# A mixture-of-experts stage with split weights, a fixed first block for each expert, and GpSimd at work on the output weights

## The reference, cut to what matters

```python
probs = softmax(ht @ w_router); sel = probs + b_router     # 512 x 16
# the best of 4 groups of experts, then the best two experts in it: e_idx, gate_w
def expert_block(args):
    xb, e = args
    return (silu(xb @ w1[e]) * (xb @ w3[e])) @ w2[e]       # w1, w3: 1024 x 512, w2: 512 x 1024
# each token's two results, weighted by gate_w, are added
```

## Time and profile before

| | |
|---|---|
| median of 3 runs | 3185.82 us (3181.49 to 3186.29) |
| the profiled execution: its own time | 3187.43 us |
| its span | 3185.7 us |
| PE busy | 2728.6 us (86%) |
| DVE, ACT, POOL busy | 1517.8, 946.5, 61.4 us |
| mean granted TensorE clock | 0.906 of full |

### The profile page before, as it was taken

The page is one execution under the profiler, slowest core; times in us unless marked ns, Lnnn a source line. Parts: engine busy times, 40 slices in busy tenths (PEclk is TensorE's granted clock), DMA queues, the critical chain, the costliest instruction groups (busy, mean ns, idle before and its releaser), DMA issues. The chain is left out here.

```text
span 3185.7 us, 32864 instructions
## 1 busy us (share of the span) xinstructions
PE 2728.6 (86%) x12575; PEld 1996.8 (63%) x12575; DVE 1517.8 (48%) x2296; ACT 946.5 (30%) x1497; POOL 61.4 (2%) x161
## 2 busy tenths in 40 slices
PE   7999799678887899389999478899999666899998
PEld 6777687556665775344444234578887665778886
DVE  6778435545656574311111444463344885453334
ACT  4333222224434322111111223353232323353233
POOL 0000000000000000100000100000000000000000
PEclk8999699889887999599999788899999887999999
DMA  7667343211210740088888201123232112222330
GB/s 241 212 218 240 130 155 143 86 53 47 53 34 27 272 151 1 31 325 309 324 304 301 83 26 43 57 71 101 93 101 71 16 30 80 80 79 93 93 106 27
DMA packets 304736, 390.75 MB, mean 123 GB/s; under 512 B 23560, under 2 KB 211451, under 8 KB 304348
## 3 DMA queue, kind: packets, MB, share of 16 engines
q1 hardware_dynamic: 295196, 354.33, 33.7%
q0 software_dynamic: 6960, 25.70, 2.1%
q10 hardware_dynamic: 2448, 8.91, 0.7%
HBM read 361.11 MB, written 27.80 MB: 122 GB/s over the span
## 5 line engine op out<-in xcount | busy, mean ns | idle before, releaser
L2887 PE MATMUL banks<-big,tail_w_parts 128*128 128x512 f32 x1920 | 442.9, 393 | 16.9 <-DVE tail_w_parts L3044 16.9
L2887 PEld LDWEIGHTS banks<-big,tail_w_parts 128*128 128x128 f32 x1920 | 363.3, 189 | 95.0 <-DVE tail_w_parts L3044 17.5
L2887 PE MATMUL banks<-h_parts_second,tail_w_parts 128*128 128x512 f32 x1440 | 333.1, 392 | 12.8 <-DVE h_parts_second L3069 12.8
L1264 PE MATMUL banks<-h_parts,ssm_w_parts 128*128 128x512 f32 x984 | 267.1, 433 | 61.6 <-DVE ys_plain L1535 26.6
L2887 PEld LDWEIGHTS banks<-h_parts_second,tail_w_parts 128*128 128x128 f32 x1440 | 272.5, 189 | 71.2 <-issue 14.4
L3044 DVE TENSOR_TENSOR tail_w_parts<-w_second,tail_w_parts 128x2048 fp32r<-128x2048 f32 x70 | 160.3, 2292 | 283.2 <-ACT tail_w_parts L2948 283.2
L1264 PEld LDWEIGHTS banks<-h_parts,ssm_w_parts 128*128 128x128 f32 x984 | 205.2, 212 | 119.8 <-DVE ssm_w_parts L1514 42.5
L2341 PE MATMUL banks<-w,experts_xt 128*128 128x512 f32 x544 | 238.9, 597 | 0.9 <-DVE experts_xt L2388 0.9
L2948 ACT ACTIVATE tail_w_parts<-w_second 128x2048 fp32r<-128x2048 f32 x70 | 133.8, 1914 | 265.4 <-PE banks L2887 265.3
L2341 PEld LDWEIGHTS banks<-w,experts_xt 128*128 128x128 f32 x544 | 104.2, 192 | 132.6 <-issue 132.6
L601 PE MATMUL banks<-h_parts,ssm_parts 128*128 128x512 f32 x576 | 135.8, 398 | 14.8 <-DVE ssm_parts L590 11.6
(11 more groups left out here) (606 smaller groups left out, 3812.7 us busy)
## 6 DMA issues: line engine op xcount, KB each, us to landing
w_second<-in_mlp_w_dram SPq DMA_DIRECT2D x64, 1024.0 KB, 5.1
w<-in_w_exp_gate_dram SPq DMA_DIRECT2D x17, 2048.0 KB, 8.9
w<-in_w_exp_up_dram SPq DMA_DIRECT2D x17, 2048.0 KB, 8.8
w<-in_w_exp_down_dram SPq DMA_DIRECT2D x17, 2048.0 KB, 10.8
w<-in_w_in_dram SPq DMA_DIRECT2D x65, 512.0 KB, 3.9
w<-in_mod_mix_w_dram SPq DMA_DIRECT2D x24, 1024.0 KB, 5.0
w<-in_mod_ffn_w_dram SPq DMA_DIRECT2D x24, 1024.0 KB, 5.0
w<-in_w_in_dram SPq DMA_DIRECT2D x16, 1024.0 KB, 6.9
```

The costliest lines, as they stand in the source:

```text
L1264: mm = pe.matmul(ps[:, t % 2, :], parts[:, t % SPLITS, w, kk, :], k.hp[:, x, kk, :], start=(kk == 0 and j == 0), stop=(kk == KD - 1 and j ...
L2887: mm = pe.matmul(ps[:, bank(n, f), :], w_part(n, w)[:, kk, f * P:(f + 1) * P], x[:, v, kk, :], start=(first_chunk(n) and kk == 0 and j == ...
```

## The change

The routing becomes one stage, and the experts' loop is written out for 16 experts, with all of their weights split.

- The router's weights and the six 1 MB halves of expert 0 are loaded during `norm_mix`. The logits are formed in `norm_ffn_in` behind each tile of `h` (8 products of 512 columns, 16 rows of output). The ranks come from `rank_entries`: five operations for all pairs at once.
- Expert n has row p of its first block at row `p * NBLK + n` of one DRAM tensor, `k.rows`; rows over 128 go to spill blocks behind these (`NBLK` = 24). POOL scatters the rows of `h` themselves (8 indirect transfers of 0.5 MB). x of expert n is then a plain load by SP; y is stored to the place of x.
- Each expert has six halves of weights: 0, 1 gate; 2, 3 up; 4, 5 down. Each half has one raw slot in `k.w` and one split slot (`parts`). ACT makes the high parts; DVE makes the low parts of 0 to 3, and POOL those of 4 and 5. A raw slot is loaded again once its low part is made.
- Spill blocks (one here) are done after the 16 experts by the old loop in plain f32, with plain loads.

The core of it (`wait_low` waits for the low part of half h of expert n; `done` is the order of the high parts):

```diff
+    def load(self, sp, n, h):
+        if n:
+            self.wait_low(sp, n - 1, h)
+        ...
+        sp.dma_start(self.raw(h)..., src...).then_inc(self.raw_loaded[h], 16)
+    def high(self, act, n, h):
+        act.wait_ge(self.raw_loaded[h], 16 * (n + 1))
+        if n and h < 4:
+            act.wait_ge(self.up_used, 4 * (n - 1) + h + 1)
+        elif n:
+            act.wait_ge(self.down_used, 2 * (n - 1) + h - 3)
+        act.activation(self.high_part(h), self.raw(h), ACT.Copy).then_inc(self.high_done, 1)
+    def low(self, eng, n, h):
+        eng.wait_ge(self.high_done, self.done[n, h])
+        eng.tensor_tensor(self.low_part(h), self.raw(h), self.high_part(h).bitcast(F32),
+                          ALU.subtract).then_inc(self.low_done if h < 4 else self.down_low, 1)
+    def products(self, pe, n, h, out, x, first, start, stop):
+        self.wait_low(pe, n, h)
+        for kk in range(KE):
+            for j, (v, w) in enumerate(((0, 0), (0, 1), (1, 0))):
+                mm = pe.matmul(out, x[:, v, first + kk, :], self.tile(h, w, kk), ...)
+        mm.then_inc(self.up_used if h < 4 else self.down_used, 1)

 experts_stage:
 sync:
+            for n in range(NE):
+                if 1 <= n and n + 1 < NE:
+                    for h in range(4):
+                        m.load(sp, n + 1, h)
+                if n + 2 < NE:
+                    sp.wait_ge(s["x_turned"], n + 1)
+                    m.load_x(sp, n + 2)
+                if n + 1 < NE:
+                    for h in (4, 5):
+                        m.load(sp, n + 1, h)
 gpsimd:
-                pool.indirect_dma_start(xg[:], None, m.h_rows, ...)
+            for n in range(NE):
+                for half in range(2):
+                    m.low(pool, n, 4 + half)
 tensor:
+            def down(n):
+                pe.wait_ge(s["hidden_low"], n + 1)
+                if n:
+                    pe.wait_ge(s["y_copied"], 2 * n)
+                for half in range(2):
+                    m.products(pe, n, 4 + half, ps[:, 5 + half, :], ht, 0, True, True)
+            turn(0)
+            for n in range(NE):
+                pe.wait_ge(s["x_low"], n + 1)
+                for slot in range(2):
+                    for h in range(2):
+                        m.products(pe, n, 2 * slot + h, ps[:, 2 + slot, :], xt, h * KE, h == 0, h == 1)
+                if n + 1 < NE:
+                    turn(n + 1)
+                if n:
+                    down(n - 1)
+                pe.wait_ge(s["hidden_done"], n + 1)
+                ...                                 # four transposes of hidden
+            down(NE - 1)
+            pe.wait_ge(s["y_copied"], 2 * NE)
 scalar:
+            high_x(0)
+            for n in range(NE):
+                if n:
+                    high_hidden(n - 1)
+                if n + 1 < NE:
+                    m.high(act, n + 1, 0)
+                    m.high(act, n + 1, 1)
+                act.wait_ge(m.up_used, 4 * n + 2)
+                act.activation(sig[:], ps[:, 2, :], ACT.Sigmoid).then_inc(s["sig_done"], 1)
+                if n + 1 < NE:
+                    m.high(act, n + 1, 2)
+                    m.high(act, n + 1, 3)
+                    high_x(n + 1)
+                for half in range(2):
+                    m.high(act, n, 4 + half)
+                    if n:
+                        copy_y(n - 1, half)
+                if n:
+                    store_y(n - 1)
+            ...                                     # the last expert, then a wait for the stores of y
 vector:
+            low_x(0)
+            for n in range(NE):
+                if n:
+                    low_hidden(n - 1)
+                if n + 1 < NE:
+                    m.low(dve, n + 1, 0)
+                    m.low(dve, n + 1, 1)
+                dve.wait_ge(s["sig_done"], n + 1)
+                dve.tensor_tensor(t[:], ps[:, 2, :], sig[:], ALU.mult).then_inc(s["gated"], 1)
+                if n + 1 < NE:
+                    m.low(dve, n + 1, 2)
+                ...
+                dve.tensor_tensor(hidden[:], t[:], ps[:, 3, :], ALU.mult).then_inc(s["hidden_done"], 1)
+                if n + 1 < NE:
+                    m.low(dve, n + 1, 3)
+                    low_x(n + 1)
+            low_hidden(NE - 1)
```

`high_x`, `low_x`, `high_hidden` and `low_hidden` split the turned x (128x1024, from PSUM) and the turned hidden (128x512, from PSUM) in the same way. The routing stage ends with SP's loads:

```diff
+            sp.wait_ge(m.scattered, 16 * 2 * TB)
+            m.load_x(sp, 0)
+            for h in range(2):
+                m.load(sp, 1, h)
+            m.load_x(sp, 1)
+            for h in range(2, 4):
+                m.load(sp, 1, h)
```

More of the change, by code:

```diff
@@ L495, in _ @@
             k.clear(sp)
+            if experts and not logits:
+                experts.load_router(sp)
+                for h in range(EH):
+                    experts.load(sp, 0, h)
         @block.tensor
@@ L504, in _ @@
                 sum_channels(k, pe, lambda c: pe.wait_ge(s["out_done"], c + 1))
+            if logits:
+                pe.wait_ge(experts.router_loaded, 32)
+                for c in range(KD):
+                    pe.wait_ge(s["out_done"], c + 1)
+                    pe.matmul(ps[0:NE, 2, :], experts.wr[:, c, :], dst[:, c, :], start=(c == 0), stop=(c == KD - 1))
         @block.vector
@@ L2053, in _, with rank_entries @@
                                                   op1=ALU.add))
-def router_stage(k, chosen, share):
+EH = 6
+HALVES = 2 * KE
+def rank_entries(step, dve, rank, above, even, val, later):
+    shape = [P, val.shape[1], EG, EG]
+    mine = val.rearrange("p g (n o) -> p g n o", o=1).to_broadcast(shape)
+    other = val.rearrange("p g (o n) -> p g o n", o=1).to_broadcast(shape)
+    step(dve.tensor_tensor(above, other, mine, ALU.is_gt))
+    step(dve.tensor_tensor(even, other, mine, ALU.is_equal))
+    step(dve.tensor_tensor(even, even, later.rearrange("p (o n) m -> p o n m", o=1).to_broadcast(shape), ALU.mult))
+    step(dve.tensor_tensor(above, above, even, ALU.add))
+    step(dve.tensor_reduce(rank, above, AX.X, ALU.add))
@@ L2071, in _ @@
             k.clear(sp)
[L2072 to L2130, removed]
-            assert step.n == ROUTER_STEPS, step.n
@@ L2192, in _ @@
             for b in range(TB):
[L2193 to L2199 removed]
+                mm = pe.transpose(ps[:, 1, b * NE:(b + 1) * NE], lt[:, b * P:(b + 1) * P], k.ident[0:NE, 0:NE])
@@ L2271, in experts_stage @@
+            step(dve.tensor_reduce(plan_f[:, 0:SPILL], passed[:], AX.X, ALU.add))
+            step(dve.tensor_scalar(plan_f[:, 0:SPILL], plan_f[:, 0:SPILL], float(NE - 1), None, ALU.min))
+            step(dve.tensor_copy(plan_f[:, SPILL:], end[0:1, NE - 1:NE]))
+            step(dve.tensor_copy(m.plan[:], plan_f[:]))
+            for h in range(4):
+                m.low(dve, 0, h)
 def experts_stage(k, m):
```

459 lines of the change are left out of this document (270 added, 189 removed).

## The result

The changed kernel takes 3256.66 us (median of 4 runs, 3253.82 to 3257.05), the kernel before 3186.06 on the same chip (3181.49 to 3188.05). The ratio is 1.022, with an interval of 1.020 to 1.024: slower by 70 us. The forecast was 3235, the range 3165 to 3300.

The account below looks back on a forecast made before the run. PE bounded the old loop at 23.2 us a block; a ring of 29.2 us a period would bound the new one. Expert 0 at 1322.6, rounds to 1744.8 and spill block at 1785.6 put the end 48.5 us later: 3235, range 3165 to 3300.

Parts of the forecast that it names:

- a ring: Experts' loop: SP's loads, ACT's high parts and POOL's low parts follow one another, a period of 29.2 us; forecast's chance 75%.
- Rival (c): Experts' loop: the ring is not closed; transfers or PE set a period of 19 us, total 3102; chance 7%.
- Rival (b): Experts' loop: POOL's low part is cheap; below 2.85 us the kernel is faster, at 2.29 it takes 3170; chance 5%.
- (e): Experts' loop: PE falls to the low clock in its pauses and stays there, 36 us a period, total 3341; chance 5%.
- Rival (d): Experts' loop: POOL and DVE block each other on each low part, 6.7 us each, 68 more, total 3303; chance 8%.
- In front of the loop: From the norm to expert 0's first product: that product starts at 1322.6, 40.7 us earlier than before.
- The logits' products: In the norm: eight products follow the tiles of h, 7.13 us from the second tile on, ending at 1284.4.
- the scatter: In front of the loop: 8 x 0.5 MB through POOL's queue take 15.1 us, with 12 and 25 as ends.
- x of expert 0: In front of the loop: its load takes 2.6 us, by the fastest 0.5 MB store; turning and split follow.
- The ring's rounds: Experts' loop: thirteen periods of 29.2 us from expert 2's half 3 landing at 1365.2 to expert 15's at 1744.8.
- From POOL's last start of the ring: End of the experts' loop: remaining steps, with 2.6 us for the last store, put the spill block's products at 1785.6.
- both low parts (8.9 us) and then five loads (15.1): Links in each round: POOL's low parts of halves 4 and 5, then SP's five 1 MB loads, one after another.

Follow-up runs that it names:

- third experiment: On the changed kernel, SP loads halves 0 to 3 of expert n+2 before halves 4 and 5 of expert n+1: 3103.42 us, 0.974 of before.
- fourth kernel, experiment 4: The changed kernel with SP's new order of loads and all low parts on VectorE: 3085.32 us, 0.968 of before.
- experiments 3 to 5: On the changed kernel: SP's new order, 3103.42 us; with all low parts on VectorE, 3085.32; on top, unused POOL subtractions, 3168.42, or memsets, 3086.24.
- second experiment, experiment 2: On the changed kernel, VectorE instead of POOL forms the low parts of halves 4 and 5, SP's order unchanged: 3223.84 us, 1.012 of before.
- experiment 6: On the changed kernel, DVE waits for the scatter before expert 0's low parts: 3256.98 us in one run.
- experiment 5: On the kernel with new load order and all low parts on VectorE, unused POOL work: subtractions, 3168.42 us; or memsets, 3086.24 us.

## Why the prediction held, and by how much each term was off

**The sign and the mechanism held.** Slower, through a ring of SP's queue, the transfers, ACT and POOL. The three experiments on it each move the time its way: more POOL work +65.7 us, less -33, the order changed -153. Rival (c), no ring, is what the third experiment produces on purpose: it forecast 3102 and that kernel takes 3103. That they agree to 1 us is luck: (c) has 133 us less than 3235, the runs 153 less than 3257. Rival (b) fell with POOL's 4.59 us. Of (e) a part is seen: the 48 products took 12.7 to 14.0 us in every round and not 11.1, since they start after a pause of PE in which the granted clock is 0.50, the lower of the two levels, 1.2 GHz (the third stretch above). The 24 products of the down weights that follow take 5.7 us, as in the fourth kernel, which has no pauses, so PE does not stay at that level. But PE waits for the ring, so this costs nothing.

**Rival (d) is a real effect that had no room here.** POOL and DVE do hinder each other, as experiments 3 to 5 show, but in the changed kernel the groups read 2.29 and 4.59 us: the ring keeps the two engines apart. The prediction gave just that reason against (d).

**Terms of the sum.** The forecast was slower by 49 us and the runs show 70. Span for span it was 3234.2 forecast and 3254.5 measured, 20.3 more:

- In front of the loop, +7.5 (1330.1 for 1322.6). The logits' products took 9.96 us and not 7.13, +2.8: they began at the low clock, where the channel sums of the earlier trace rows ran at full clock throughout (windows as above; the clock is the seventh value):

```profile
1278.59:1283.00 4.41, 4.41 (x6) 0.86 (x7) 3.23 (x6) 4.41 (x7) 0.00 (x0) 0.50 0.00 0
1285.00:1288.55 3.55, 3.55 (x9) 0.64 (x7) 0.00 (x0) 0.00 (x0) 0.00 (x0) 1.00 0.00 0
```

- Still in front of the loop: the scatter took 17.3 us and not 15.1, +2.2: here DVE forms low parts of expert 0 beside four of the issues, where in the stretch of the earlier trace rows only two of the eight were longer, at 1.15 and 1.71 us, once DVE had started on the gathered rows. x of expert 0 took 4.7 us from its load's start (1321.08) to its first use (1325.79), where I took 2.6 from the fastest store of the earlier trace rows, +2.1; loads of expert 1's weights had been started right behind it. 1.25 is drift ahead of the change (the channel sums start at 1258.99, before at 1257.74). The copy and turning of the logits and the hand-overs give 0.9 back. DVE's 51 small steps were forecast at 13.5 us and took 13.6.
- The ring's rounds, +7.4: fourteen of 29.70 us instead of 29.2 are 7.0, and 0.4 since the sum has only 28.8 for the first. Two of three take 29.2 to 29.6, every third 30.5; in the longer ones a load in the middle of the burst lands about 1 us later. Why every third, I did not find.
- From POOL's last start of the ring (1764.59) to the spill block's first product, +3.4: 39.3 us for 35.9 in sum. The last store of y is most of it: from its start (1796.46) to ACT's copy that waits for it (1803.15) it is 6.7 us, where I again took the fastest store's 2.6, +4.1; the other steps took 0.7 less. The spill block itself +1.6: its first 32 products took 15.41 us where the earlier trace rows have 13.90. The rest is 0.4.

**The links held, but not what a faster POOL would bring.** I put both low parts (8.9 us) and then five loads (15.1) into the ring, 24.0. The trace of the changed kernel has 9.12 for the low parts and 15.4 from there to ACT's start on half 3 in the round shown, 24.6, and transfers that all but stop between half 4 and half 5. What I wrote of rival (b) does not hold: that a faster POOL gives back two low parts a round in full. In the second experiment the first came back in full and the second to a third. There half 5 is released early enough that the transfers do not stop, and the six loads with y's store among them take 19.6 us; that these set the limit is read from the transfers, no run isolates it. That kernel has 2.24 us an operation, on VectorE, and was still slower than before: 3223.84 us, where I had worked out 3170 for POOL at that speed. Of the 54 us between, 20 are the terms above and some 15 DVE's later start (1.1 us a round); the rest, by estimate, is this link. A faster POOL itself can't be tried.

**What the profile was to show.** SP waits at halves 4 and 5 for POOL and the bursts run at about 400 GB/s, as written. POOL is busy for 131 us more, for 142: its 32 operations take 146.2, but other work of it fell away. PE is busy for 70% of the loop and not 60.

**Where the gain went.** The change earns 33 us in front of the loop, and the fourth kernel shows 5.5 us a block to be had in it (23.2 against 17.73). The ring turns these into a loss of 6.5 a round.

## What to carry to other kernels

A load that stands in a queue behind a wait for another engine's result makes that engine part of the path, however little it is busy: write down for each queue what stands behind each wait, and close the circle on paper, before you ask which engine is full. Then change the order first; it was worth 153 us here, a faster engine 33. For a transfer on the path take the time of one with as much traffic beside it, not the fastest in the trace. And of two steps with two inputs, do not give one to GpSimd to relieve VectorE without looking at the mean time of VectorE's own group afterwards.

## What the runs showed of the hardware that was not expected

- POOL's indirect transfers took 0.96 to 1.11 us to issue each, and 1.89 to 2.82 while DVE formed low parts with two inputs in SBUF; the whole scatter took 17.30 us then and 13.35 without them (experiment 6). The Trainium skill, in the section named above, says that such a VectorE operation was not seen to stall GpSimd's descriptor generation. These rows say otherwise for indirect transfers, and the measurement decides. The edit moved only DVE's low parts, and all issues fell to 0.96 to 1.11. An indirect transfer also takes its slots from SBUF, and whether it was that reading or the descriptors that had to wait no run here shows.
- A subtraction of 1024 elements on POOL took 3.96 us beside a busy DVE, against 2.3 by the line through the earlier trace rows, and lengthened DVE's from 2.29 to 3.32 us; 160 memsets lengthened nothing (experiment 5).
- Six loads of 1 MB in one queue took 20.4 us in the mean from the first issue to ACT's start on the last when the second was released 4.5 us after the first, and 19.6 when it was released after 2.2 and a 0.5 MB store ran among them (experiment 2).
- One core with loads of 1 MB from one queue, and the loads of x and stores of y among them, kept 399 GB/s over 230 us (experiment 4).
- A transfer of 0.5 MB that took 2.6 us at its fastest in the kernel before took 4.7 and 6.7 us at the two places where the changed kernel waits for one, with loads of weights in flight (terms of the sum).
